# A row ring of 13 slots in place of 10, four diagonals in place of eight, and one product per slice of mixing in a streaming encoder layer with expert lookup

## What is computed

```python
oa = band_attention_prompt(qa, ka, va, rel_bias[l])
s_fin, ob = hgrn2_prompt(qb, kb, vb, logf)
...
merged = jax.nn.sigmoid(gate_a) * (oa @ w_a) + jax.nn.sigmoid(gate_b) * (ob @ w_b)
h = x + merged @ w_out
return h + peer(rmsnorm(h, norm_ffn), w_query, sub_keys, u_tab, v_tab)
...
hid = jax.nn.gelu(jnp.einsum('nd,nhkd->nhk', xb, u_tab[ib]).astype(jnp.float32), approximate=False)
return jnp.einsum('nhk,nhkd->nd', (gb * hid).astype(v_tab.dtype), v_tab[ib])
```

## Time and profile before

| | us |
|---|---|
| median of three runs | 4541.51 |
| lowest and highest run | 4533.14, 4547.78 |
| the profiled execution | 4581.09 |
| its span, from first to last instruction | 4579.2 |
| first gather issued (within the span) | about 455 |
| PE, DVE, POOL, ACT busy in the span | 3201.9, 3105.0, 2656.9, 837.2 |
| granted TensorE clock, mean | 0.787 |

### The profile page before, as it was taken

The page is one execution under the profiler, slowest core; times in us unless marked ns, Lnnn a source line. Parts: engine busy times, 40 slices in busy tenths (PEclk is TensorE's granted clock), DMA queues, the critical chain, the costliest instruction groups (busy, mean ns, idle before and its releaser), DMA issues. The chain is left out here.

```text
span 4579.2 us, 36423 instructions
## 1 busy us (share of the span) xinstructions
PE 3201.9 (70%) x11064; PEld 1997.1 (44%) x11064; DVE 3105.0 (68%) x6491; ACT 837.2 (18%) x2078; POOL 2656.9 (58%) x2349
## 2 busy tenths in 40 slices
PE   4968558896787567976874578858765677675555
PEld 3847314463464235643651256636432345343211
DVE  0142995647749976578579856685699765858865
ACT  1221112212111123121111222211111122111100
POOL 0001565646746676667456756575577765856776
PEclk7769657598888678987986698979876788787677
DMA  5415657989999899999998999989999999999998
GB/s 126 134 49 180 171 152 187 242 256 339 339 325 371 307 348 343 380 333 322 345 352 318 335 328 375 347 315 348 333 368 348 367 384 369 359 384 359 355 379 329
DMA packets 531664, 1408.39 MB, mean 308 GB/s; under 512 B 47952, under 2 KB 223568, under 8 KB 530704
## 3 DMA queue, kind: packets, MB, share of 16 engines
q0 software_dynamic: 317856, 1149.91, 70.2%
q1 hardware_dynamic: 211088, 246.98, 16.7%
q10 hardware_dynamic: 2528, 9.18, 0.5%
HBM read 1385.98 MB, written 19.92 MB: 307 GB/s over the span
## 5 line engine op out<-in xcount | busy, mean ns | idle before, releaser
L857 PE MATMUL PS<-ring,diag 128*128 128x512 f32 (+1 forms) x2304 | 1551.9, 814 | 963.8 <-DMA ring<-in_peer_v,idx 736.1
L557 POOL DMA_INDIRECT ring<-in_peer_v,idx x1152 | 1338.1, 1162 | 762.1 <-PE PS L857 394.1
L557 POOL DMA_INDIRECT ring<-in_peer_u,idx x1152 | 1300.6, 1129 | 721.9 <-DVE hid L1557 343.0
L1557 DVE CUSTOM_DVE_ANT_0 ring<-ring,xt 128x1024 f32<-128x1024 f32 (+1 forms) x1152 | 1397.7, 1221 | 416.3 <-DMA ring<-in_peer_u,idx 271.4
L857 PEld LDWEIGHTS PS<-ring,diag 128*128 128x128 f32 (+1 forms) x2304 | 503.0, 238 | 1733.5 <-issue 1548.6
L573 PE MATMUL PS<-xnT,wring 128*128 128x256 f32 (+2 forms) x3840 | 775.8, 364 | 131.4 <-DMA wring<-in_w_in 60.2
L1567 DVE SCALAR_TENSOR_TENSOR acc<-ring,wk,acc 128x1024 f32<-128x1024 f32 (+1 forms) x576 | 739.4, 1284 | 119.5 <-DMA ring<-in_peer_v,idx 86.1
L573 PEld LDWEIGHTS PS<-xnT,wring 128*128 128x128 f32 x3840 | 692.7, 202 | 251.3 <-issue 154.2
L543 POOL DMA_DIRECT2D xt<-xn_scr x9 | 5.5, 607 | 419.1 <-DMA xn_scr<-arena 419.0
L1173 ACT ACTIVATE diag<-ident,wk 128x128 f32<-128x128 f32 (+1 forms) x576 | 189.2, 384 | 73.4 <-issue 28.7
L577 PE MATMUL PS<-wring,xnT 128*128 128x256 f32 (+1 forms) x864 | 194.6, 384 | 8.0 <-DMA wring<-in_w_in 7.9
(11 more groups left out here) (179 smaller groups left out, 2620.3 us busy)
## 6 DMA issues: line engine op xcount, KB each, us to landing
wring<-in_w_in SPq DMA_DIRECT2D x110, 1024.0 KB
wring<-in_peer_query SPq DMA_DIRECT2D x40, 1024.0 KB
wring<-in_w_out SPq DMA_DIRECT2D x20, 1024.0 KB
ring<-in_peer_u,idx POOLq DMA_INDIRECT x1152
ring<-in_peer_v,idx POOLq DMA_INDIRECT x1152
bias<-rel_scr SPq DMA_DIRECT2D x80, 144.0 KB
wring<-in_w_branch_a SPq DMA_DIRECT2D x10, 1024.0 KB
wring<-in_w_branch_b SPq DMA_DIRECT2D x10, 1024.0 KB
```

Of the source, the lines that this page charges most:

```text
L557: pool.indirect_dma_start(ring[0:tile_rows[tn], n % R, :], None, u_tab if kind == "u" else v_tab, bass.IndirectOffsetOnAxis(ap=idx[0:tile_ ...
L857: mm = pe.matmul(PS[0:rows, 6 + half, :], diag[0:rows, seq % ND, 0:rows], ring[0:rows, n % R, 512 * half:512 * (half + 1)], start=(h == 0 ...
L1557: dve.tensor_tensor_reduce(row, row, xt[0:rows, s, :], 1.0, 0.0, ALU.mult, ALU.add, hid[0:rows, m % 2, k:k + 1]).then_inc(dve_used, 1)
```

## The change

Three slots are added to the ring (R = 13, 12 KB on each partition). The room is taken from four places: `idx` and `gates` hold the lists of four tiles in place of nine, tile t at t % 4 (the lookup of a tile is over before the list of the fourth tile after it is written); the sample's new keys and values stand in slot 1 of the prompt's key and value tiles, which tile 1 takes in the next group; and ND, the number of diagonals, goes from 8 to 4, so ACT makes diagonal j at step 2j-2 of its head and not at step 2j-6 (PE uses it at step 2j+1 in both). Second, the slices of stages B, D, E, G and H hold one product in place of two, with half the cost each; in stage F the block of subtractions is cut into three slices and the masking of the scores stands in a slice of its own. The computation is the same.

```diff
-R = 10
-ND = 8
+R = 13
+ND = 4
+LISTS = 4
...
-    b = [3.5] * (4 + nt) + [2.0]
+    b = [1.7] * (8 + 2 * nt) + [2.0]
     c = [1.8] * (2 * (HA * nt + 3))
-    d = [1.5] + [2.5] * 8 + [0.5]
-    e = [3.5] * (4 + 2 * nt) + [0.5]
-    f = ([8.0, 4.5, 2.0] + [2.3, 1.5, 3.2] * HB + [1.0, 0.5, 2.0, 1.5]) * nt
-    gg = [2.5] * 8 + [0.5]
-    h = [3.5] * (2 * nt) + [0.5, 2.5, 0.5, 1.5, 3.0] + [1.5] * nt
+    d = [1.5] + [1.3] * 16 + [0.5]
+    e = [1.7] * (8 + 4 * nt) + [0.5]
+    f = ([2.5, 2.5, 3.0, 4.5, 2.0] + [2.3, 1.5, 1.2, 2.0] * HB + [1.0, 0.5, 2.0, 1.5]) * nt
+    gg = [1.3] * 16 + [0.5]
+    h = [1.7] * (4 * nt) + [0.5, 2.5, 0.5, 1.5, 3.0] + [1.5] * nt
...
-        kS = sb("kS", [P, CB, DEC])
-        vS = sb("vS", [P, DA])
+        kS = kT[:, :, P:P + DEC]
+        vS = v[:, 1, :]
...
-        idx = sb("idx", [P, NT * P], U32)
-        gates = sb("gates", [P, NT * P])
+        idx = sb("idx", [P, LISTS * P], U32)
+        gates = sb("gates", [P, LISTS * P])
...
                 for i, n in enumerate(by_stage[g, "B"]):
                     product(n, xnT)
-                    if i % 2:
-                        yield
+                    yield
...
-                        if k == max(0, TOPK // len(ON_PE) * j - 6):
+                        if k == max(0, TOPK // len(ON_PE) * (j - ND // 2 + 1)):
                             make_diag(m - 2, j)
...
-                for i, n in enumerate(by_stage[g, stage]):
-                    if products[n][4] == "branch":
-                        late.append(n)
-                    if i % 2:
-                        for q in late[:-2]:
-                            gate(q)
-                        now = late[-2:] if products[n][4] == "branch" else []
-                        if not now:
-                            for q in late:
-                                gate(q)
-                        late = now
-                        yield
+                for n in by_stage[g, stage]:
+                    for q in late:
+                        gate(q)
+                    late = [n] if products[n][4] == "branch" else []
+                    yield
...
                         dve.tensor_tensor(e4[:, :, :, 1, :], c4[:, :, :, 1, :], ref, ALU.subtract)
                         dve.tensor_tensor(e4[:, :, :, 0, :], ref, c4[:, :, :, 0, :], ALU.subtract)
+                        if lev in (1, 3):
+                            yield
...
-                for i_ in range(0, len(hn), 2):
+                for i_ in range(len(hn)):
                     if i_:
-                        add_out(hn[i_ - 2])
                         add_out(hn[i_ - 1])
                     yield
-                add_out(hn[-2])
                 add_out(hn[-1])
```

More of the change, by code:

```diff
@@ L555, in _ @@
                     pool.wait_ge(dve_used if who == "dve" else pe_used, seq + 1)
-                at = tn * P + h * TOPK + k
+                at = tn % LISTS * P + h * TOPK + k
                 pool.indirect_dma_start(
@@ L723, in mix @@
                     nch = rows // CH
-                    yield
-                    yield
+                    for _ in range(4):
+                        yield
                     if ti == 0:
@@ L948, in mix @@
                     i.then_inc(pj_free[n % 2], 1)
-                    if i_ % 2:
-                        yield
+                    yield
                 kt = kt_before[g]
@@ L1042, in mix @@
                     i.then_inc(pj_free[n % 2], 1)
-                    if i_ == 7:
+                    if i_ == 6:
                         act.wait_ge(f_fg, g + 1)
                         act.activation(Q[:, :, 0:W], K2[:, :, 0:W], ACT.Ln).then_inc(f_ln, 1)
-                    if i_ % 2:
-                        yield
+                    yield
                 leave()
@@ L1105, in mix @@
                 enter(act, g, "H")
-                for _ in range(2 * nt + 1):
+                for _ in range(4 * nt + 1):
                     yield
@@ L1287, in mix @@
                 enter(dve, g, "B")
-                for _ in range(4 + nt):
+                for _ in range(8 + 2 * nt):
                     yield
@@ L1343, in mix @@
                 for i_, n in enumerate(en):
[L1344 to L1350, removed]
+                    if 1 <= i_ <= HB:
+                        h = i_ - 1
+                        n = en[h]
+                        dve.wait_ge(pj_free[n % 2], n // 2 + 1)
+                        i = dve.tensor_scalar(K2[:, h, 0:W], Q[:, h, 0:W], one_lb[:, h:h + 1], lb[:, h:h + 1],
+                                              ALU.mult, ALU.add)
+                        if i_ == HB:
                             i.then_inc(f_fg, 1)
-                    if i_ == 9:
+                    if i_ == 8:
                         dve.wait_ge(f_ln, g + 1)
@@ L1406, in mix @@
                         at = PS[:, b0:b0 + 2, :].rearrange("p a (b t) -> p (a b) t", t=P)[0:rows, 0:NL + 1, 0:rows]
-                        link(dve.tensor_tensor(Am[0:rows, :, 0:rows], at, masks[0:rows, :, 0:rows], ALU.mult))
+                        i = dve.tensor_tensor(Am[0:rows, :, 0:rows], at, masks[0:rows, :, 0:rows], ALU.mult)
+                        yield
+                        link(i)
                         if fh >= 2:
@@ L1541, in unit @@
                     rows = tile_rows[m // PH]
+                    at = m % (LISTS * PH) * TOPK
                     dve.wait_ge(e_gelu, m + 1)
@@ L1545, in unit @@
                     dve.tensor_tensor(wk[0:rows, m % 2, :], glu[0:rows, m % 2, :],
-                                      gates[0:rows, m * TOPK:(m + 1) * TOPK], ALU.mult).then_inc(e_w, 1)
+                                      gates[0:rows, at:at + TOPK], ALU.mult).then_inc(e_w, 1)
                 elif kind == "R":
```

11 lines of the change are left out of this document (4 added, 7 removed).

## The result

| | before | changed |
|---|---|---|
| median of the runs, us | 4537.75 (4 runs) | 4457.82 (4 runs) |
| lowest and highest | 4533.14, 4547.78 | 4451.06, 4460.97 |
| the profiled execution | 4581.09 | 4459.93 |

The ratio is 0.9818, with a 95% interval of 0.9804 to 0.9833: 80 us less, or 1.8%. Forecast were 74 us less and 4467 us. The profiled execution of before lies some 43 us over its median and that of the changed kernel 2 us, so the two traces differ by 121 us where the medians differ by 80.

What follows compares the result with a forecast made beforehand. No one bound: a ring of ten slots, full at some times and empty at others, between POOL with DMA and DVE with PE. Terms: -57 - 17 - 10 + 10 = -74 us, so 4467 us; range 4390 to 4555.

Steps and rivals of the forecast that it cites:

- the ring: Three more slots between POOL's gathers and the consumers DVE and PE: two terms, 57 us and 17 us less.
- DVE's starving: DVE's waits for u and v rows: to fall from 357 to under 300 us.
- The term of 57 us: Stretches 1000 to 1400, 2000 to 2400, 3000 to 3200 us: DMA share rises to 0.98, saving 29, 16 and 12 us.
- The 17 us for the ends of top-k stretches: Four top-k stretches end with 13 landed rows in place of ten, so the next stretch starts 4.3 us ahead.
- POOL's waits: POOL's waits for free ring slots: to fall from 745 us to some 500.
- One product a slice: Single products in place of pairs let PE find PSUM halves freed earlier: 10 us less.
- DVE's wait for products: DVE's 116.3 us of waits for PE's products could grow by 116 us at the most.
- The cut subtractions: Stage F's 13 subtractions in three pieces: costed at 0, as ten slots cover the block; 51 us at most.
- Diagonals: Four diagonals leave ACT at most three steps behind PE's need: 10 us more, between none and 36.
- Rival B: Slower by the diagonals, with PE's waits for them over 330 us: 4585 us, chance 0.12.
- Rival A: The supplier, POOL, is itself the limit, so the gain is small or none: 4530 to 4555 us, chance 0.13.
- Rival C: Full ring stalls also in pieces costed at 0: 130 to 200 us less, 4375 us, chance 0.15.

Runs made afterwards that it cites:

- ring_only: The kernel before with 13 ring slots, four diagonals, short lists and the sample's keys in slot 1, but its old slices: 4467.23 us, ratio 0.9860.
- slices_only: The changed kernel with ten slots and eight diagonals, so the new slices without the deeper ring: 4508.94 us, ratio 0.9950.
- r13_nd6: The changed kernel with six diagonals in place of four, made at step 2j-4: 4458.96 us, ratio 0.9823.
- f_split_alone: The kernel before with nothing but the cut of stage F's 13 subtractions into three slices: 4516.45 us, ratio 0.9969.

## Why the prediction was right, and where its steps were not

**The total and the ring.** -74 us were forecast for the slots and +10 for the diagonals, so -64 together; ring_only, which has both, measured -62 (53 to 73 from its interval). The mechanism held: POOL's slot waits and the consumers' starving fell together, and DVE's starving came out under the 300 us that were named. How the ring's gain was spread over the stretches did not hold. The term of 57 us was worked out for a DMA share of 0.98 in three stretches; they reached 0.94, 0.94 and 0.93, and the term's own formula gives 13 + 0 + 2 = 15 us for these. The 17 us for the ends of top-k stretches were of the right kind and somewhat small: stage B lies close behind them, and over four groups it took 203 us in slices_only and 177 to 182 in the changed kernel. More came where I had taken no term: 9 to 14 us in I, 5 or 6 in the tail. That the ring's terms add up to what was measured is therefore partly luck.

**POOL's waits.** I expected some 500 us and found 634, with another 102.6 for lists of experts not yet selected (52.8 before). Most of POOL's slot waits belong to stretches in which PE or DVE is the bound. There a deeper ring only moves the wait, as the prediction said of the earlier trace rows. The size of a supplier's wait was a poor measure of what a buffer can earn.

**One product a slice.** Forecast -10; at thirteen slots one pair of kernels gives 3 us less and the other 3 us more, so nothing is found, though 10 us are not excluded. PE's waits for DVE's additions, five in number, stayed five:

```profile
PE PS L578 <- DVE arena L1445: 34.3, 5, 8.5
```

Each group has one, so they belong to one place of stage H and not to the boundaries of pairs; that they are stage entries, as the prediction suspected, is not shown. DVE's wait for products grew from 116.3 to 146.9 us, in the direction that was bounded by +116, and no loss of time from it is seen.

**The cut subtractions.** This is the step of the sum that failed: I cost them at 0, with 51 us as the most, on the ground that ten slots hold 14 us of POOL's work. They were worth 7 to 21 us at ten slots and 10 to 22 at thirteen, across sets. The condition was named (a ring that comes in full) and the rows of stage F would have told: POOL waited for DVE there 13.0 us in the third group, while it was busy or issuing for 164 of 178 us. This term was too low by 10 to 22 us and the single products too high by about 10; with the ring's -62 the sum comes to -72 to -84, around the 80 measured. So the total was hit partly by luck: two errors that nearly cancelled, and a ring term whose parts were wrong and whose sum was right.

**Diagonals.** Forecast +10, bounds 0 to 36; r13_nd6 gives 0 and the pair at twelve slots 8. PE's waits rose by 65 us, under the 250 that were named, and the cause is the deeper ring and not the short lead. ACT's own wait for PE (135.4 us), which is the price of only four buffers, I had not named; r13_nd6 took 77 us of it away and was no faster. Rival B is out: its point was 330 us, and 237 were found.

**Rival A** is partly right: POOL's 0.3 + 1.14 us a row is what bounded stage F before, and the fourteenth slot is worth nothing. But the ring could still carry rows from stages where POOL waits into those where it has no time to. The issue of a gather did not lengthen: 1143 ns against 1146 in the mean, and 137.24/120 = 1.14 us in the top-k stretch against 1.18. **Rival C**'s sign, a share over 1.0 from 1000 us to the end, is not there: it is 0.96. What it said of the subtractions, that the ring stalls there, came true, at 10 to 22 us in place of 51. The 358 GB/s of the Trainium skill ("DMA: Bandwidth & Descriptors", "Where 436 GB/s comes from") do not bind here: the tail of the changed kernel runs at 400 GB/s for 238 us.

## What to carry to other kernels

A deeper ring between a steady supplier and uneven consumers is worth what it can carry from stretches bound by a consumer into stretches bound by the supplier; look for the stretch in which the supplier is busy nearly all the time, and ask how many of its instructions could have run before it, what stops it inside, and how far the next engine's own work is behind. Waits of the supplier elsewhere say little. And look inside such a stretch for long uncut pieces of a consumer's work: a cut there cost a few lines and earned 0.2 to 0.5%, while finer slices in stretches bound by the consumer earned nothing that could be measured. Last, a profile that lies 1% over its median puts its excess into single stages: compare kernels that differ in one thing and whose profiles lie near their medians.

## What was not expected of the hardware

The rate of the gathers in the tail differs between executions of equal work. There, where nothing but the lookup runs, the changed kernel moved 400 GB/s at a DMA share of 1.02. In the profile of before the same work stood at 369 GB/s and 0.98, and in slices_only and f_split_alone, with ten slots too, at 393 and 390 GB/s:

```profile
4300.80:4560.50 259.70, 150.09 (x212) 49.20 (x212) 168.55 (x224) 19.26 (x61) 192.65 (x181) 0.75 0.98 369
```

The number of instructions is nearly the same (POOL 181 in both), and POOL's mean is 1.01 against 1.06 us. Other kernels with ten slots needed 243 to 245 us for it and those with eleven or more 238 to 240, so some 6 us come from the ring and the rest is that execution's own. What slowed it, the traces don't show. The stair of eleven and thirteen slots, if it is one, is the other thing that they leave open.
